# Hybrid encoder trunk: the banded attention's four value products in one TensorE block, its second turning one quarter earlier

## The reference

```python
ya = swa_sink_attention(qa, ka, va, a_sinks) * jax.nn.silu(ga)       # banded attention, 8 heads of 64
za = ya @ w_oa
yb = rmsnorm(gla_chunk_readout(...), b_head_g) * jax.nn.silu(gb);  zb = yb @ w_ob
yc = mla_attention(q_nope, q_rope, k_nope, k_rope, v_c) * jax.nn.silu(gc);  zc = yc @ w_oc
y = m[:, :, 0] * za + m[:, :, 1] * zb + m[:, :, 2] * zc              # m: sigmoid gates of x
return x + y @ w_out
```

## Time and profile before

| what | value |
|---|---|
| median of 3 runs | 931.62 us (931.48 to 931.8) |
| span of the profiled execution, first to last instruction | 929.7 us |
| median less that span | 1.9 us |
| TensorE busy | 922.0 us (99%) |
| DVE busy | 601.2 us (65%) |
| ACT busy | 387.2 us (42%) |
| mean granted TensorE clock | 0.999 |

### The profile page before, as it was taken

How to read it: one execution, slowest core, us unless ns; L and a number is a source line. 1 busy time by engine, 2 the same in 40 slices (tenths; PEclk the granted TensorE clock), 3 DMA queues, 4 the chain that set the end, 5 groups by cost and what they waited for, 6 DMA issues and landing times.

```text
span 929.7 us, 13082 instructions
## 1 busy us (share of the span) xinstructions
PE 922.0 (99%) x5108; PEld 755.8 (81%) x5108; DVE 601.2 (65%) x982; ACT 387.2 (42%) x724; POOL 0.2 (0%) x4
## 2 busy tenths in 40 slices
PE   9999999999999999999999999999999999999997
PEld 7988888888888777888889888888888887778886
DVE  7856467448757877575457664674477568876834
ACT  7453344324543454432444333442264425562324
POOL 0000000000000000000000000000000000000000
PEclk9999999999999999999999999999999999999999
DMA  7324324322434255422232333253234433454542
GB/s 292 136 70 147 114 69 136 113 91 80 140 122 140 85 151 150 145 92 90 91 113 91 95 108 106 68 163 109 91 92 143 140 114 109 122 156 136 146 127 90
DMA packets 43789, 110.98 MB, mean 119 GB/s; under 512 B 8592, under 2 KB 11408, under 8 KB 43600
## 3 DMA queue, kind: packets, MB, share of 16 engines
q1 hardware_dynamic: 39664, 104.82, 35.8%
q10 hardware_dynamic: 4064, 5.33, 2.2%
HBM read 85.41 MB, written 2.23 MB: 94 GB/s over the span
## 4 chain that ended last, share of the span: by engine, by line
PE 86%; DVE 5%; ACT 3%; SPq 2%; issue 1%; DMA 1%; ACTq 1%; DVEq 0%
PE ring L657 65%; PE nat L657 9%; PE nat L868 3%; PE aux L892 2%; SPq L495 1%; DVE w_lo L1215 1%; ACT work L1117 1%; PE nat L672 1%; PE nat L671 1%; PE nat L673 1%; DVE work L1514 1%; DMA raw<-pieces 1%; ACT w_hi L909 1%; PE ring L672 1%; PE ring L671 1%
## 5 line engine op out<-in xcount | busy, mean ns | idle before, releaser
L657 PE MATMUL ring<-act_hi,w_hi 128*128 128x512 f32 x784 | 308.7, 394 | 0.0
L657 PE MATMUL ring<-act_lo,w_hi 128*128 128x512 f32 x784 | 305.5, 390 | 0.0
L657 PE MATMUL ring<-act_hi,w_lo 128*128 128x512 f32 x784 | 305.2, 389 | 0.0
L909 ACT ACTIVATE w_hi<-raw 128x1024 fp32r<-128x1024 f32 x152 | 161.7, 1064 | 340.5 <-PE ring L657 275.5
L1215 DVE TENSOR_TENSOR w_lo<-raw,w_hi 128x1024 fp32r<-128x1024 f32 x152 | 184.6, 1216 | 82.7 <-ACT w_hi L909 82.3
L657 PEld LDWEIGHTS ring<-act_hi,w_hi 128*128 128x128 f32 x784 | 147.1, 188 | 38.2 <-issue 8.4
L657 PEld LDWEIGHTS ring<-act_hi,w_lo 128*128 128x128 f32 x784 | 147.2, 188 | 31.1
L657 PEld LDWEIGHTS ring<-act_lo,w_hi 128*128 128x128 f32 x784 | 147.2, 188 | 29.7
L1545 DVE SCALAR_TENSOR_TENSOR gates<-ring,rstd 128x512 f32<-128x512 f32 x72 | 49.3, 685 | 77.0 <-PE ring L657 76.8
L657 PE MATMUL ring<-y_hi,w_hi 128*128 128x512 f32 x192 | 74.9, 390 | 0.0
L657 PE MATMUL ring<-y_hi,w_lo 128*128 128x512 f32 x192 | 74.7, 389 | 0.0
(11 more groups left out here) (227 smaller groups left out, 995.6 us busy)
## 6 DMA issues: line engine op xcount, KB each, us to landing
raw<-pieces SPq DMA_DIRECT2D x152, 512.0 KB, 3.5
bank_g<-work SPq DMA_DIRECT2D x120, 64.0 KB, 2.0
lat<-work SPq DMA_DIRECT2D x72, 64.0 KB, 2.0
bank_g<-work ACTq DMA_DIRECT2D x40, 64.0 KB, 2.2
xt<-x_t SPq DMA_DIRECT2D x8, 256.0 KB, 4.9
bank_a<-work SPq DMA_DIRECT2D x32, 64.0 KB, 2.0
bank_g<-bank_a SPq DMA_DIRECT2D x16, 128.0 KB, 3.9
out<-gates SPq DMA_DIRECT2D x7, 256.0 KB, 2.1
```

Of the source, the lines that this page charges most:

```text
L657: mm = pe.matmul(dst, stationary, moving, start=start and i == 0, stop=stop and i == 2)
L909: nc.scalar.activation(w_hi[:, n % HL, :], raw[:, n % RAW, :], ACT.Copy).then_inc(hi_split.sem, 1)
```

## The change

Query blocks 0 to 3 are multiplied in one TensorE block of 64 matmuls at place 56, into four banks (`aux`, `nat[0]`, `nat[1]`, `nat[2]`), waiting for both groups' DMAs. Gates, `y_hi` and `y_lo` of blocks 0 and 1 move from places 45 to 50 to places 56 to 60, those of blocks 2 and 3 from 56 to 60 to 60 to 64. `turn_a` 2, `divide_a` 3 and `turn_a` 3 stand one quarter sooner, and `send` 1 too. The list now ends with `("y_lo", 3)`.

```diff
-        (45, ("values_a", 0), ("gate_a", 0)),
-        (46, ("y_hi", 0), ("turn_a", 2)),
-        (47, ("y_lo", 0), ("divide_a", 3), ("turn_a", 3), ("gate_a", 1)),
-        (48, ("send", 1), ("y_hi", 1)),
-        (50, ("y_lo", 1)),
-        (56, ("values_a", 2), ("gate_a", 2)),
-        (57, ("y_hi", 2)),
-        (58, ("y_lo", 2), ("gate_a", 3)),
-        (59, ("y_hi", 3)),
-        (60, ("y_lo", 3))))
+        (45, ("turn_a", 2)),
+        (46, ("divide_a", 3), ("turn_a", 3)),
+        (47, ("send", 1)),
+        (56, ("values_a", 0), ("gate_a", 0)),
+        (57, ("y_hi", 0)),
+        (58, ("y_lo", 0), ("gate_a", 1)),
+        (59, ("y_hi", 1)),
+        (60, ("y_lo", 1), ("gate_a", 2)),
+        (61, ("y_hi", 2)),
+        (62, ("y_lo", 2), ("gate_a", 3)),
+        (63, ("y_hi", 3)),
+        (64, ("y_lo", 3))))
...
-    behind = [("turn_a", 1), ("turn_a", 3), ("turn_c", 0), ("values_a", 2)] + [("value_c", y) for y in range(len(C_SETS) - 2)]
+    behind = [("turn_a", 1), ("turn_a", 3), ("turn_c", 0), ("values_a", 0)] + [("value_c", y) for y in range(len(C_SETS) - 2)]
...
-        o_t2 = nat[0].rearrange("p (f n) -> p f n", f=BR)
+        o_a = [o_t, *(nat[i].rearrange("p (f n) -> p f n", f=BR) for i in range(3))]
...
                     elif name == "values_a":
-                        if i == 0:
-                            pe.wait_ge(v_shifted.sem, v_shifted.at(layer, 32))
-                            pe.wait_ge(aux_free.sem, aux_free.at(layer, len(AUX)))
-                            pe.wait_ge(exp_done.sem, exp_done.at(layer, NA))
-                        else:
-                            pe.wait_ge(o_read.sem, o_read.at(layer, i))
-                        pe.wait_ge(turned_placed.sem, turned_placed.at(layer, 16 * TURN_PARTS * (i // 2 + 1)))
-                        value_a(i, o_t).then_inc(value_done.sem, 1)
-                        value_a(i + 1, o_t2).then_inc(value_done.sem, 1)
+                        pe.wait_ge(v_shifted.sem, v_shifted.at(layer, 32))
+                        pe.wait_ge(aux_free.sem, aux_free.at(layer, len(AUX)))
+                        pe.wait_ge(exp_done.sem, exp_done.at(layer, NA))
+                        pe.wait_ge(turned_placed.sem, turned_placed.at(layer, 32 * TURN_PARTS))
+                        for t in range(TT):
+                            value_a(t, o_a[t]).then_inc(value_done.sem, 1)
...
-                out = o_t2 if i in (1, TT - 1) else o_t
+                out = o_a[i] if i < TT else o_t
```

## The result

The changed kernel takes 933.33 us (median of 21 runs, 932.36 to 933.75) against 931.78 for the kernel before beside it (931.48 to 932.16): ratio 1.0016, 95% interval 1.001 to 1.0022. It is slower by 1.55 us, 0.17%, less than the 0.2% named as the bound of a measurable change, though the interval lies above 1. Measured again beside other runs it gave 933.15 against 931.88, 1.27 us more, ratio 1.0014 (1.0005 to 1.0023). The forecast was 932.9, 1.26 us more. The profiled span is 931.3 us, 1.6 more than before.

What follows compares the result with a forecast made beforehand. TensorE, busy 922.0 of 929.7 us, was taken as the bound. A layer: -2.11 + 1.78 + 0.59 + 0.37 = +0.63; both layers +1.26, so 931.62 + 1.26 = 932.9 us, range 931.0 to 934.2.

Steps and rivals of the forecast that it cites:

- The removed block and the 32 more matmuls: TensorE, places 45 and 56: removal saves 2.11 us a layer, 32 more matmuls add 1.78; 0.33 is getting in and out.
- The wait for the sends: TensorE at the merged block, place 56: waits 0.87 us for group 1's sends instead of 0.28, so +0.59 a layer.
- the rival of the long burst: SP's queue between turn_a 3 and the merged block: a burst of 8.14 us adds 0.65 a layer, 934.2 in all; 24%.
- the sign of the long burst: Profile after, merged block: a TensorE wait over 1.2 us would prove the forecast burst length of 7.49 us wrong.
- The forecast's case: SP's group 1 bursts: start 1.2 us sooner and take 7.49 us, giving a wait of 0.87 a layer; forecast itself 50%.
- The quarter sooner that moves nothing: DVE's queue: two transpositions a quarter sooner in the list change nothing; two instructions leaving the queue bring 1.2 us in all.
- Piece 46: TensorE's fourth output waits for ACT's copy, as the tanh now runs ahead of it: +0.37 us a layer; no wait, 12%.
- The clock: TensorE: a 0.9 us wait could lower 2.4 to 1.2 GHz, costing 5.4 us a layer for one piece, 943.8; 1%.
- The cover: Work hidden behind TensorE: ACT's rounding of piece 44 slips from 250.63 to some 253.6, its low part still in time.

Runs made afterwards that it cites:

- h_split_look: Profile of the kernel before with group 1's sends split 10 (SP) and 6 (ACT); this execution took 931.58 us, the timed kernel 931.21, ratio 0.9994.
- c_both: Changed kernel with the tanh put back behind piece 46 and group 1's sends split 10 and 6: 930.59 us, ratio 0.9986 to the kernel before.
- b_split: Changed kernel with group 1's sixteen sends split 10 (SP) and 6 (ACT) instead of 12 and 4: 931.29 us, ratio 0.9993 to the kernel before.
- d_late: Changed kernel with the tanh behind piece 46 and the merged block one quarter later, at place 57: 930.68 us, ratio 0.9987 to the kernel before.
- after_again: The changed kernel unaltered, measured and profiled again: 933.15 us against 931.88 for the kernel before; its profiled execution took 933.60.
- f_turn_alone: Kernel before, two value blocks kept, with turn_a 2, divide_a 3, turn_a 3 and send 1 a quarter sooner: 931.19 us, ratio 0.9994.
- a_tanh: Changed kernel with tanh 23 put back behind piece 46: 932.58 us against 931.91 for the kernel before, ratio 1.0007; a profiled execution took 932.18.
- g_tanh_alone: Kernel before with only its last list entry, tanh 23, left ahead of piece 46: 932.34 us, ratio 1.0006.
- e_oldturn: Changed kernel with turn_a 2, divide_a 3, turn_a 3 and send 1 back at places 46 to 48: 933.07 us against 931.8, ratio 1.0014.
- c_again: Changed kernel with tanh behind piece 46 and sends split 10 and 6, measured again: 930.62 us, ratio 0.9986 to the kernel before.

## Why the prediction was right, point by point

**The removed block and the 32 more matmuls.** Forecast -2.11 + 1.78. The 48 into `nat` take 2.74 us to the next usual matmul (261.59 to 264.33), 0.057 each with the way out of the block among it, so the 0.0556 held; h_split_look shows the 2.11, and c_both beside it shows 3.86 for one block against 4.22 for two, 0.36 where the forecast had 0.33. The 81 ns of the Trainium skill ("TensorE: Matmul & The Clock Gate", section "Back-to-back issue gap") are not met by these matmuls, whose weights are 128x64. By that figure the merged block of 64 would take some 5.2 us, an estimate, and it takes 3.64 (260.69 to 264.33). The forecast chose the row.

**The wait for the sends** was the term that decides, and is shown from both sides: take two sends off SP's burst (b_split, where 0.11 is left in one layer, and c_both, where nothing is) or ask 1.36 us later (d_late), and it is gone. Forecast 0.87 a layer. The block could have begun 0.227 + 0.09 after the last usual matmul, at 259.58 and 718.75; it began at 260.69 and 719.57, so the wait measured 1.11 in the first layer and 0.82 in the second. In the second layer each part was hit: the burst took 7.49 and started 1.28 sooner (6.27 behind piece 40's emptying, before 7.55). In the first layer the burst took 7.77, as one of its sends took 0.86 us to issue where the median is 0.59. That is short of the 7.81 from which the rival of the long burst was to decide. In after_again the same burst of the same kernel took 8.35, and the profile gives a wait of 1.59, over the 1.2 that was named as the sign of the long burst:

```profile
251.25 8.35 SPq L497 DMA_DIRECT2D bank_g<-work  x12
...
261.14 1.09 PE L737 MATMUL aux<-bank_g,bank_a 128*64 128x128 f32 x16 [1.59 <-DMA bank_g<-work]
```

So the rival came true in the first layer of one of the two profiled executions of the changed kernel, at the place and at about the price that it named (8.35 - 7.49 = 0.86 more); that execution took 933.60. The forecast's case, both bursts short, was seen in neither. The 0.3 us between the profile's 1.24 and the first measurement's 1.55 may well be executions with a longer burst. Their bursts are not on record. The spread agrees with it without showing it: the 21 executions of the changed kernel lie within 1.39 us, those of the kernel before beside them within 0.68; in versions without this wait 11 executions lie within 0.53 (d_late), 0.81 (c_both) and 1.17 (f_turn_alone).

**The quarter sooner that moves nothing** held for the last transposition: 5.57 us against 5.58 from piece 40's emptying to the last transposition, with and without it, and 6.83 (251.58 - 244.75) against 6.81 in the kernel before. What brings it forward by 1.26 is that `gate_a` 0 and `y_lo` 0 left DVE's queue. The forecast did not price that the low part of piece 43 comes later, and with it the load of piece 46, though its rival of the long burst named that load.

**Piece 46.** Forecast 0.37 a layer, measured 0.31 in the trace; a_tanh lies 0.60 below the changed kernel's 1.27, and g_tanh_alone 0.54 above the kernel before. The term was a little too large: TensorE began the fourth output at 277.73, 0.33 and not 0.37 late.

**Luck.** That the forecast of 1.26 and the profile's 1.24 agree to 0.02 is partly chance. The merged blocks cost 0.10 more than forecast (0.46 + 0.16 against twice 0.26) and piece 46 0.12 less (twice 0.31 against twice 0.37), and the profiled execution of after_again, the same kernel, shows 1.78.

**The clock** stayed full through the waits: the stretch with the wait of 1.04 us reads

```profile
259.40:260.60 1.20, 0.25 (x2) 0.00 (x0) 0.69 (x1) 0.85 (x1) 0.00 (x0) 1.00 0.51 101
```

with a granted clock of 1.00 (the third figure from the end), 2.4 GHz, and from the tenth usual matmul behind the block on the starts are 0.227 us apart again (six steps from 266.51 to 267.87). **The cover** that was named held too: ACT's rounding of piece 44 came at 254.48 instead of 250.63, later than the forecast 253.6 because ACT's four sends took 2.99 and not 2.46, and no wait of TensorE for a low part arose there.

## What to carry to other kernels

On an engine that never idles, merging two blocks gives back only what getting in and out costs, here 0.33 us a time, and the engine then reaches its next wait sooner by all that was removed ahead of it: look first at what that wait is for and when it is ready. Moving steps up in a list did not bring the last of them forward on an engine with a backlog; what counted was which instructions left the queue ahead of it. But it changes the order of those between, and so when a buffer comes free and a load starts: look at these too. An edit that takes "the last entry" of a list takes another one when the list grows, so name the entry.

## What had not been expected

The length of group 1's burst, which SP issues one send after the other, is not fixed. The traces show where it grows: in each case in a single send, where most take 0.59 us to issue.

With ACT's sends beginning 1.24 us behind SP's, both layers of all three such kernels (the kernel before, g_tanh_alone, h_split_look) have one send of SP's that takes 0.84, and the burst of twelve takes 7.79 to 7.81. With ACT beginning together or 0.64 behind, one of ACT's sends takes 0.87 or more instead, and SP's burst takes 7.48 to 7.50 where nothing else disturbs it. TensorE waits for SP's last send, which lands last, so it matters on which queue the long one falls; that fits the gain of f_turn_alone. Why there is such a send was not tried.

A second lengthening is in the first layer alone. In the versions in which the load of piece 46 is issued 3.24 us ahead of the burst (248.15 and 251.39 in the changed kernel), one of SP's sends takes 0.86 to 1.46 us: the bursts of twelve took 7.77, 8.35, 7.93 and 8.02 (the changed kernel, after_again, a_tanh_look, d_late), and that of ten in b_split 6.78. In the changed kernel the longest is this:

```profile
L497 SPq DMA_DIRECT2D bank_g<-work x12: 513/591/864, 251.4 to 258.6; - x12
```

(shortest, median and longest issue in ns), and after_again has 1461 as its longest. There the load lands just after the burst has begun, 3.4 us behind its issue in the changed kernel (251.55 and 251.39). In e_oldturn and f_turn_alone the load is issued 4.43 and 3.84 ahead and has landed when the burst begins, and the first layer's burst takes 7.49 and 7.50. But the load is not enough to explain it: c_both and c_again have the same 3.24 with bursts of ten of 6.26, and the second layer of the changed kernel has it too (707.31 and 710.55) with a burst of 7.49. So the long bursts were seen only where that load was still landing, in five of seven first layers and in no second one. What else it takes stays open.
